# A ring of four 4 MB weight homes and a transposed gather of two experts at once, in the mixture-of-experts loop of a hybrid decoder step

## What is computed

```python
def moe(h, w_router, b_router, w_gate_up, b_gate_up, w_down, b_down):
    logits = (xt @ w_router + b_router).astype(jnp.float32)
    top_v, top_i = lax.top_k(logits, TOP_K)          # 4 of 32
    gate = jax.nn.softmax(top_v, axis=-1)
    ...
    def expert_block(args):
        xb, e = args
        gu = xb @ w_gate_up[e] + b_gate_up[e]        # 1024 x 2048
        gt, up = gu[..., :D_EXPERT], gu[..., D_EXPERT:]
        gt = jnp.minimum(gt, SWIGLU_LIMIT)
        up = jnp.clip(up, -SWIGLU_LIMIT, SWIGLU_LIMIT)
        act = (up + 1) * (gt * jax.nn.sigmoid(gt * SWIGLU_ALPHA))
        return act @ w_down[e] + b_down[e]           # 1024 x 1024
```

## Time and profile before

| | us |
|---|---|
| median of 3 runs | 1392.07 (1383.91 to 1394.49) |
| the profiled execution, its own time | 1394.99 |
| its span in the trace | 1393.2 |
| start of the first expert's gate/up on TensorE | 460.23 |
| end of the last expert's down projection | 1379.80 |
| last weight issue by SyncE | 1336.8 |
| TensorE busy (share of the span) | 1316.5 (94%) |
| VectorE, ScalarE busy | 377.2 (27%), 259.2 (19%) |
| bytes moved | 459.93 MB, 330 GB/s over the span |

### The profile page before, as it was taken

One profiled execution on the slowest core, in us unless ns is written; L12 is line 12 of the kernel. 1 busy time (PEld: TensorE's weight loads), 2 busy tenths in 40 slices (PEclk: granted clock), 3 DMA queues, 4 the chain that ended last, 5 costly groups with the idle time before them and its releaser, 6 DMA issues.

```text
span 1393.2 us, 16949 instructions
## 1 busy us (share of the span) xinstructions
PE 1316.5 (94%) x6704; PEld 627.8 (45%) x6704; DVE 377.2 (27%) x705; ACT 259.2 (19%) x473; POOL 79.6 (6%) x48
## 2 busy tenths in 40 slices
PE   6999969798889999999999999999999999999996
PEld 5888846797745333333333333333333333333332
DVE  3043765975453211111112111121112111121112
ACT  2113433122202111111111111121111111111112
POOL 0000151360000000000000000000000000000001
PEclk9999978898897899999999999999999999999998
DMA  8356673013458699999999999999999999999994
GB/s 263 133 158 166 227 210 79 4 44 124 156 188 341 247 415 428 429 428 429 428 429 428 429 429 429 429 429 428 429 429 429 429 428 429 428 429 428 429 429 168
DMA packets 52505, 459.93 MB, mean 330 GB/s; under 512 B 7922, under 2 KB 10300, under 8 KB 27884
## 3 DMA queue, kind: packets, MB, share of 16 engines
q1 hardware_dynamic: 49252, 451.45, 78.6%
q0 software_dynamic: 1888, 5.34, 2.0%
q10 hardware_dynamic: 1328, 2.64, 0.6%
HBM read 454.27 MB, written 5.11 MB: 330 GB/s over the span
## 4 chain that ended last, share of the span: by engine, by line
PE 83%; DMA 6%; DVE 4%; issue 3%; ACT 2%; POOL 1%; SPq 1%; ACTq 0%; DVEq 0%; POOLq 0%
PE ps L1688 30%; PE ps L1715 15%; PE ps L1290 8%; PE ps L1651 4%; PE ps L1636 4%; PE ps L1673 4%; PE ps L1421 3%; DMA work<-in_w_gate_up 2%; DMA ring<-in_w_gate_up 2%; PE ps L1549 2%; PE ps L1265 2%; PE ps L1643 2%; ACT work L703 1%; DVE ring L826 1%; PE ps L1490 1%
## 5 line engine op out<-in xcount | busy, mean ns | idle before, releaser
L1688 PE MATMUL ps<-ring,work 128*64 128x512 f32 x1536 | 338.5, 596 | 2.5 <-DMA ring<-in_w_gate_up 1.6
L1688 PEld LDWEIGHTS ps<-ring,work 128*64 128x64 f32 x1536 | 108.3, 137 | 229.3 <-issue 225.1
L1715 PE MATMUL ps<-ring,work 128*64 128x512 f32 x768 | 170.1, 595 | 0.0
L1290 PE MATMUL ps<-work,ring 128*128 128x264 f32 x672 | 152.0, 389 | 0.4 <-DVE work L826 0.4
L1200 DVE TENSOR_SCALAR work<-ps 128x512 f32<-128x512 f32 x32 | 22.2, 692 | 437.1 <-PE ps L1688 437.1
L1290 PEld LDWEIGHTS ps<-work,ring 128*128 128x128 f32 x672 | 128.6, 192 | 22.7 <-DVE work L826 0.5
L1218 DVE SCALAR_TENSOR_TENSOR work<-work 128x512 f32<-128x512 f32 x32 | 24.1, 752 | 348.1 <-ACT work L735 348.1
L1688 PE MATMUL ps<-work 128*64 128x512 f32 x512 | 113.2, 594 | 0.5 <-DMA work<-in_w_gate_up 0.5
L1715 PEld LDWEIGHTS ps<-ring,work 128*64 128x64 f32 x768 | 53.0, 137 | 115.4 <-issue 115.4
L726 ACT ACTIVATE work<-work 128x512 f32<-128x512 f32 x32 | 20.2, 632 | 442.6 <-DVE work L1200 442.6
L826 DVE TENSOR_TENSOR work<-work 128x512 f32<-128x512 f32 (+8 forms) x79 | 62.4, 790 | 52.7 <-ACT work L518 46.7
(11 more groups left out here) (263 smaller groups left out, 1086.6 us busy)
## 6 DMA issues: line engine op xcount, KB each, us to landing
ring<-in_w_gate_up SPq DMA_DIRECT2D x96, 2048.0 KB, 21.5
ring<-in_w_down SPq DMA_DIRECT2D x48, 2048.0 KB, 25.7
work<-in_w_gate_up SPq DMA_DIRECT2D x32, 2048.0 KB, 22.2
work<-in_w_down SPq DMA_DIRECT2D x16, 2048.0 KB, 26.3
ring<-in_w_in SPq DMA_DIRECT2D x6, 3072.0 KB, 15.8
ring<-in_w_out SPq DMA_DIRECT2D x1, 4096.0 KB, 14.3
ring<-in_w_in SPq DMA_DIRECT2D x2, 1536.0 KB, 8.7
ring<-in_cache_k SPq DMA_DIRECT2D x16, 192.0 KB, 3.3
```

Source lines behind the costliest of these rows:

```text
L1290: last = mm(psum(job, T), WIN[gi % 2][:, k, j * 128:(j + 1) * 128], hT[:, k, :], start=k == 0, stop=k == KD - 1)
L1688: last = mm(PS[bnk][g * 64:g * 64 + 64, :], lhs, UNIT[n % 8][:, w0 + base + g * 512:w0 + base + (g + 1) * 512], start=False, stop=k == KD - 1)
L1715: last = mm(PS[BY][g * 64:g * 64 + 64, :], lhs, UNIT[n % 8][:, w0:w0 + 512], start=k == 0, stop=k == KD - 1)
```

## The change

**Homes and pieces.** The ring becomes four homes of 4 MB at the same total of 16 MB. A unit of gate/up is 4 rows of 8 KB for each partition, 32 KB in a row; two units an expert. The down weights of an expert are one unit, of two pieces of 16 KB for each partition, as before. Three units an expert, twelve in a group of four experts. `unit_used` is raised once a unit, so twice in gate/up, and once at the end of down. Before the loop it is raised 1, 2 and 1 times at the three places.

**Halves.** Of the twelve units of a group, n = 4 (the second gate/up unit of expert 1) goes out as two DMAs of 2 MB, the first as soon as TensorE has used the first half of unit 0 (`half_used`). Unit n = 11 (the down unit of expert 3) goes out as two DMAs with a semaphore each, so TensorE can begin on its first half.

**Gather.** `sel` now holds two experts side by side (128 tokens x 128 slots), made by VectorE at every second expert with four instructions in place of two at each. A gather is a matmul with the normed rows, every fourth column, as the stationary operand and `sel` as the moving one: its result is transposed already. One half of D for two experts is 8 matmuls of 128x128; half 0 is done in the even expert and half 1 in the odd one, for the next pair. `gather_T`, its semaphores and the copy to `xg` go; ScalarE makes one copy a half, into one of two buffers `XG`.

**Order.** The transposes of the activations and their copy now come ahead of those of the gating matrix. The four bias matmuls of the next expert stand together after down, in an order in which neighbours differ in rows and columns of the array. Between router and loop `open_sum(0)` is split: one half ahead of the wait for the gates, the other after the ranks. VectorE adds the samples' bias before it makes the gates of the prompt, and the gates' transposes use bank BY. All rows of D are spread over the partitions by four instead of by two, in the router's weights too.

The diff, cut to its core:

```diff
-        UNIT = [view(RING, 4096 * 5, 4096), view(RING, 4096 * 4, 4096), view(RING, 4096 * 3, 4096), view(RING, 4096 * 2, 4096),
-                view(WORK, 13256, 4096), view(WORK, 24504, 4096), view(RING, 0, 4096), view(RING, 4096, 4096)]
+        UNIT = [view(RING, 8192 * 2, 8192), view(RING, 8192, 8192), view(WORK, 20408, 8192), view(RING, 0, 8192)]
...
-        xg = place(512)
-        xgT = place(4, 128)
+        XG = [place(2, 4, 2, SLOT), view(WORK, 17576, 2, 4, 2, SLOT)]
...
-            def load_experts(first, it):
+            def load_experts(first, it, turn4):
 
                 for j in range(4):
-                    for u in range(6):
-                        n = 6 * j + u
-                        sp.wait_ge(S_("unit_used"), it * 6 + n + 1)
-                        if u < 4:
-                            src = wgu[bass.ds(first + j, 1), u * 256:(u + 1) * 256, :].rearrange("a (p j) n -> p (a j n)", j=2)
+                    for u in range(3):
+                        n = 3 * j + u
+                        unit, done = UNIT[n % 4], S_(f"ld_u{n % 4}")
+                        if u < 2:
+                            src = wgu[bass.ds(first + j, 1), u * 512:(u + 1) * 512, :].rearrange("a (p j) n -> p (a j n)", j=4)
                         else:
-                            src = wdn[bass.ds(first + j, 1), (u - 4) * 512:(u - 3) * 512, :].rearrange("a (p j) n -> p (a j n)", j=4)
-                        sp.dma_start(UNIT[n % 8], src).then_inc(S_(f"ld_u{n % 8}"), 16)
+                            src = wdn[bass.ds(first + j, 1)].rearrange("a (u p j) n -> p (a u) (j n)", u=2, j=4)
+                            unit = unit.rearrange("p (u m) -> p u m", u=2)
+                        if n == 4:
+                            sp.wait_ge(S_("half_used"), turn4 + 1)
+                            sp.dma_start(unit[:, 0:4096], src[:, 0:4096]).then_inc(S_("ld_half"), 16)
+                        elif n == 11:
+                            sp.wait_ge(S_("unit_used"), it * 3 + n + 1)
+                            sp.dma_start(unit[:, 0:1], src[:, 0:1]).then_inc(S_("ld_down_half"), 16)
+                        sp.wait_ge(S_("unit_used"), it * 3 + n + 1)
+                        rest = slice(1 if n == 11 else 0, 2) if u == 2 else slice(4096 if n == 4 else 0, 8192)
+                        sp.dma_start(unit[:, rest], src[:, rest]).then_inc(done, 16)
...
+            def gathered(P, half, count):
+
+                act.wait_ge(S_("xg_full"), count)
+                nc.scalar.activation(XG[P % 2][:, half, :, :, OWN:SLOT],
+                                     PS[BX][:, :].rearrange("p (c e s) -> p c e s", c=4, e=2)[:, :, :, OWN:SLOT], ACT.Copy)\
...
+                with act.Fori(0, NE // 4) as q:
+                    for j in range(4):
+                        it = act.snap(p * NE + q * 4 + j)
+                        act.wait_ge(S_("gt"), it + 1)
+                        nc.scalar.activation(sg, gt, ACT.Sigmoid, scale=ALPHA).then_inc(S_("sg"), 1)
+                        gathered(j // 2 + 1, j % 2, it + 3)
+                        act.wait_ge(S_("actT_full"), it + 1)
+                        nc.scalar.activation(actT, PS[BG][:, :].rearrange("p (c s) -> p c s", c=4), ACT.Copy).then_inc(S_("actT_out"), 1)
+                        act.wait_ge(S_("selgT_full"), it + 1)
+                        nc.scalar.activation(selgT, PS[BY][:, 0:256], ACT.Copy).then_inc(S_("selgT_out"), 1)
+                        act.wait_ge(S_("samp_out"), it + 1)
+                        act.wait_ge(S_("unit_used"), it * 3 + 7)
+                        nc.scalar.activation(yS, PS[BY][:, :], ACT.Copy).then_inc(S_("y_out"), 1)
...
+                        if e_ == 0:
+                            for n in range(4):
+                                v.tensor_scalar(sel[:, n // 2, n % 2, :], C["slots"][:, 0:SLOT], posx[:, n // 2, bass.ds(it + 2 + n % 2, 1)], None,
+                                                ALU.is_equal).then_inc(S_("sel_next"), 1)
...
-            pe.sem_inc(S_("unit_used"), 3)
+            pe.sem_inc(S_("unit_used"), 1)
...
-            pe.sem_inc(S_("unit_used"), 3)
+            pe.sem_inc(S_("unit_used"), 2)
...
-            pe.sem_inc(S_("unit_used"), 2)
+            pe.sem_inc(S_("unit_used"), 1)
...
+            open_sum(1, 0)
+            open_sum(1, 1)
             h2_T(2)
             logits(1)
+            open_sum(0, 0)
             pe.wait_ge(S_("gate"), 1)
...
-            open_sum(0)
...
+            open_sum(0, 1)
...
-            def gather(sem_name, count):
-                pe.wait_ge(S_(sem_name), count)
-                for m in range(2):
-                    for g in range(2):
-                        last = mm(PS[BX][g * 64:g * 64 + 64, :], sel[:, m, :], h2[:, m, g * 512:(g + 1) * 512],
-                                  start=m == 0, stop=m == 1)
+            def gather(half):
+
+                for c in range(4):
+                    for m in range(2):
+                        last = mm(PS[BX][:, c * 128:(c + 1) * 128], h2[:, m, half * 512 + c:(half + 1) * 512:4],
+                                  sel[:, m].rearrange("p e s -> p (e s)"), start=m == 0, stop=m == 1)
                 last.then_inc(S_("xg_full"), 1)
 
-            def gather_T(it):
-                pe.wait_ge(S_("xg_out"), it + 1)
-                for c in range(4):
-                    last = nc.tensor.transpose(PS[BX][:, c * 128:(c + 1) * 128], half(xg, c // 2, c % 2), C["ident"])
-                last.then_inc(S_("xgT_full"), 1)
-
-            def bias(i, count):
+            def bias(count):
 
                 pe.wait_ge(S_("pick"), count)
-                for g in range(2):
+                for i, g in ((0, 0), (1, 1), (0, 1), (1, 0)):
                     q = slice(i * NE, (i + 1) * NE)
                     mm(PS[(BG, BU)[i]][g * 64:g * 64 + 64, :], pick[q, :], ebias[q, g * 512:(g + 1) * 512], start=True, stop=False)
 
-            gather("sel", 1)
+            pe.wait_ge(S_("sel"), 1)
+            gather(0)
             bank_free(BU)
             bank_free(BG)
             pe.wait_ge(S_("ld_ebias"), 32)
-            bias(0, 1)
-            bias(1, 1)
-            gather_T(0)
+            bias(1)
+            pe.wait_ge(S_("xgT_out"), 1)
+            gather(1)
...
                 pe.wait_ge(S_("xgT_out"), it + 1)
                 for k in range(KD):
-                    n, w0 = 6 * j + k // 2, (k % 2) * 2048
-                    if k % 2 == 0:
-                        pe.wait_ge(S_(f"ld_u{n % 8}"), turn4 * 48 + 16 * (n // 8 + 1))
+                    if k == 4 and j % 2 == 0:
+                        pe.wait_ge(S_("xgT_out"), it + 2)
+                    n, w0 = 3 * j + k // 4, (k % 4) * 2048
+                    if k % 4 == 0:
+                        if n == 4:
+                            pe.wait_ge(S_("ld_half"), turn4 * 16 + 16)
+                        pe.wait_ge(S_(f"ld_u{n % 4}"), turn4 * 48 + 16 * (n // 4 + 1))
                     h_, c_ = k // 4, k % 4
-                    lhs = xgT[:, c_, h_ * 64:h_ * 64 + 64]
+                    lhs = XG[j // 2][:, h_, c_, j % 2, :]
                     for bnk, base in ((BG, 0), (BU, 1024)):
                         for g in range(2):
                             last = mm(PS[bnk][g * 64:g * 64 + 64, :], lhs,
-                                      UNIT[n % 8][:, w0 + base + g * 512:w0 + base + (g + 1) * 512], start=False, stop=k == KD - 1)
-                    if k % 2:
+                                      UNIT[n % 4][:, w0 + base + g * 512:w0 + base + (g + 1) * 512], start=False, stop=k == KD - 1)
+                    if k == 1 and j == 0:
+                        last.then_inc(S_("half_used"), 1)
+                    if k % 4 == 3:
                         last.then_inc(S_("unit_used"), 1)
                 combine(it)
-                gather("sel_next", it * 2 + 2)
+                if j % 2 == 0:
+                    pe.wait_ge(S_("sel_next"), it * 2 + 4)
+                pe.wait_ge(S_("xgT_out"), it + 2)
+                gather(j % 2)
+                pe.wait_ge(S_("act"), it + 1)
+                for c in range(4):
+                    last = nc.tensor.transpose(PS[BG][:, c * 128:(c + 1) * 128], up[:, c:512:4], C["ident"])
+                last.then_inc(S_("actT_full"), 1)
                 pe.wait_ge(S_("selg"), it * 2 + 2)
                 for m in range(2):
                     last = nc.tensor.transpose(PS[BY][:, m * 128:(m + 1) * 128], selg[:, m, :], C["ident"])
                 last.then_inc(S_("selgT_full"), 1)
-                gather_T(it + 1)
-                pe.wait_ge(S_("act"), it + 1)
-                for c in range(4):
-                    last = nc.tensor.transpose(PS[BG][:, c * 128:(c + 1) * 128], up[:, c:512:4], C["ident"])
-                last.then_inc(S_("actT_full"), 1)
-
-                bias(1, it + 2)
+
                 pe.wait_ge(S_("selgT_out"), it + 2)
                 pe.wait_ge(S_("actT_out"), it + 1)
+                n = 3 * j + 2
+                if j == 3:
```

(25 more changed lines are left out.)

122 lines of the change are left out of this document (50 added, 72 removed).

## The result

The changed kernel takes **1415.51 us** (median of 4 runs, 1412.76 to 1418.67), the one before, run beside it, 1389.52 (4 runs, 1383.91 to 1394.49): a ratio of 1.018, 95% interval 1.015 to 1.021. Slower, where 1390 (1381 to 1400) was forecast. The profiled execution took 1415.79 (span 1413.8), 20.8 over that of before, 1394.99.

The account below looks back on a forecast made before the run. DMA was taken as the bound: last idling, then bytes over rate, then TensorE's tail. Issue +2.6, rate -7.1 and tail +2.4 summed to -2.1 us, giving 1390.0 us on the median's scale, range 1381 to 1400.

Parts of the forecast that it names:

- The gather: Between gate/up and down: 8 matmuls of 128x128 at 0.27 us each, 2.1 us, bounds 1.9 to 4.5.
- X: TensorE's time from the end of gate/up to down in each expert: 5.8 us, against 6.72 before.
- The bound: In the loop: DMA binds; TensorE's period of 27.7 us stays under the 28.6 at which the periods cross.
- Rival (c): In the loop: TensorE becomes the bound through a gather above 3.1 us; 1437 us at the 4.5 bound; chance 6%.
- The rate: Gate/up DMA from unit 6 on: 32 KB pieces save 14.8 ns fixed cost a piece, -7.1 us.
- Issue and start: Loop's beginning: first expert starts at 460.5; the issue ending DMA's idling moves to 488.8, +2.6 us.
- rival (b): Before the first expert: the clock stays up or rises earlier, -6.5 us, 1383.5; chance 16%.
- The tail: From the last gate/up unit's landing to the end of down: 19.8 us against 17.4, +2.4 us.
- The biases: After each expert's down: all four bias matmuls together take 1.0 us.
- What would show it: Trace signs: 431 to 432 GB/s, period 27.7 then 29.1 us, TensorE waiting about 1.5 us at second gate/up units.
- Rival (e): In the loop: TensorE's DMA waits of about 1.5 us an expert drop the clock; not priced, no chance given.

Follow-up runs that it names:

- a1_contig: The changed kernel with h2 stored sorted by VectorE, so the gather reads its stationary operand without a stride: 1391.41 us, ratio 0.9996 to the kernel before.
- five f32 loads above: Gather's stationary load at steps of 4, 8, 12, 16 and 32 bytes, in five kernels, the changed one among them: 192, 196, 262, 330 and 335 ns.
- e6_stride3: `a1_contig` with the gather's stationary operand read at a step of three f32 elements (wrong columns, same work): 1395.73 us, one run.
- a4_contig_16k: `a1_contig` with gate/up in 16 KB pieces instead of 32 KB and h2 sorted by two: 1398.86 us, ratio 1.0055 to the kernel before.
- b1_halves: `a1_contig` with units 6 and 10 of each four experts also fetched in halves: 1391.98 us, ratio 1.0003 to the kernel before.
- b2_gather_only: The kernel before, its ring kept, with only the change's two-expert gather (stride two), new order and biases together: 1386.06 us, ratio 0.9967.
- bf16 runs: `a1_contig` with the gather reading h2 and sel as bf16 at steps of 4, 8, 16 bytes (wrong columns): 1389.89, 1393.32, 1387.39 us, one run each.
- a2_16k_stride2: The changed kernel with gate/up in 16 KB pieces, so the gather reads every second column: 1393.59 us, ratio 1.0016 to the kernel before.
- a3_ring_only: The kernel before with only the change's ring of four 4 MB homes and its pieces, old gather kept: 1394.42 us, ratio 1.0023.
- e5_stride8: `a1_contig` with the gather's stationary operand read at a step of eight f32 elements (wrong columns, same work): 1413.02 us, one run.

## Why the prediction was wrong, point by point

- **The gather, the step that failed.** It was 2.1 us (bounds 1.9 to 4.5), is 3.94 to 4.01, near the upper end. The row taken, had shape, type and engine right, and columns side by side. The row that seemed to clear the stride, the activations' transposes, was of another kind. At the same step its load takes 213 ns, the gather's 330; the gating transposes of the same kernel, whose columns lie side by side, load in 147 ns:

```profile
L1708 PEld LDWEIGHTS ps<-work x128: 196/213/302, 480.5 to 1391.9; 128*128 128x128 f32 x128
```

```profile
L1712 PEld LDWEIGHTS ps<-work 128*128 128x128 f32 x64 | 8.4, 147 | 0.0
```

  So the step has its price there too, but hardly in the spacing of the records, which is all that the prediction looked at: transposes follow each other by 0.12 us with the step and by 0.11 without. The gather's records follow each other by 0.11 us side by side (`a1_contig`) and by 0.23 at a step of four. Its spacing grows with its load at every step: 0.11, 0.12, 0.17, 0.23 and 0.24 us for the five f32 loads above. Why a transpose pays so much less than a matmul for the same step stays open.
- **X, gate/up to down.** Forecast 5.8, after 7.28 to 7.55; at the right price of the gather the forecast would have been 5.8 + 3.94 - 2.1 = 7.6. With no stride it is 5.34 and 5.53, so the copies behind the gather were put 0.3 to 0.4 too dear: from its end to down it is 1.4 us (510.21 + 1.40 = 511.61), not 1.8. ScalarE starts each copy before the last has ended: at 510.21, 510.68 and 511.18, for 0.54, 0.60 and 0.38 us.
- **The bound.** Rival (c), held at 6%, is what happened. Its threshold, periods crossing at 28.6 us, fits the runs on either side: `e6_stride3` at 28.4 ends on a DMA wait, the change at 29.39 on TensorE. Loop start 460.98 + 32 x 29.39 - 1.02 = 1400.4, which the trace has at 1400.3: 20.5 later than before, the 20.8 of the result. The error was in one input and its chance, not in the mechanism.
- **The rate.** This term was mis-sized too: -7.1 us forecast, -3.7 measured (`a1_contig` against `a4_contig_16k`), and in the changed kernel nothing of it shows, since DMA doesn't bind. Two sizes, one of them from another tensor with other rows, don't give the slope between the next two.
- **Issue and start.** Forecast 460.5 and 488.8, measured 460.98 and 489.6: near, but in part by luck, since errors cancel. The two gathers took 4.03 and 3.93 instead of 3.6, and X was 1.7 longer; against that the clock was up for expert 0's gate/up (13.91 for 15.52), which rival (b) had in part.
- **The tail** was 19.8, and `a1_contig`, where DMA binds, has 19.5. **The biases** were 1.0, measured 1.02.
- **What would show it.** "I am wrong if TensorE never waits for DMA after the middle of the loop" was the right test, and was met.
- **Rival (e)**, waits that drop the clock, did not arise in the change, where TensorE never waits for DMA in the loop. It did in `b1_halves` (last section).

## What to carry to other kernels

Before a weight layout is made for longer DMA pieces, look at what it does to the step with which TensorE reads the *other* operand: at 16 bytes or more a f32 stationary load went from 192 to 330 ns, and with matmuls of 128 columns their spacing doubled. Whether longer matmuls would hide it no run here shows. Take the price of a new access pattern from a row with that pattern in the same kind of instruction; where no such row exists, the chance of the far bound is not 6%. And when two engines' periods stand within 3% of each other, a busy share or a rate in GB/s can't tell which is the bound: the releaser of the first matmul of a unit and the time from issue to landing can.

## What the runs showed of the hardware

- The load at a step of four f32 doesn't follow TensorE's clock. In the change, at a granted clock of 0.50 (443 to 460 us), both gathers' 16 loads took 3.81 us in all, and 3.81 at 1.00. Side by side they do: `a1_contig`'s 16 loads ahead of the loop, at 0.50, took 3.49 us where 16 at full clock took 1.86. At 0.50 steps of two (`b2_gather_only`) and three (`e6_stride3`) took the same 3.49, so at the lower clock only the step of four stood out, and by 9%.
- The clock can fall around a wait for DMA. In `b1_halves` TensorE waits 2.7 us for a gate/up unit five times in the loop, and at three of these, within 1 us of where it resumes, the granted clock falls to 0.50 for 3.4 us:

```profile
914.00:918.00 4.00, 1.27 (x8) 0.37 (x6) 0.00 (x0) 0.00 (x0) 0.00 (x0) 1.00 1.02 434
918.00:922.00 4.00, 4.00 (x12) 1.37 (x11) 0.00 (x0) 0.00 (x0) 0.00 (x0) 0.57 0.98 418
```

  The traces with f32 gathers whose longest wait is 1.9 us or less, `a1_contig` with 22 waits over 0.9 us among them, show no such fall in the loop. The bf16 runs, whose longest waits are 2.5 us, have 9 to 12 such stretches, and two of the five waits of `b1_halves` have none, so the length of a wait is not all that decides.
- The start of the loop scatters by 15 us between profiled executions, 450.3 to 464.8, and the clock ahead of it goes with that in part. Windows of `a2_16k_stride2` (its loop starts at 455.9) and of `a1_contig` (463.1):

```profile
444.00:452.00 8.00, 7.72 (x54) 4.77 (x53) 5.80 (x28) 2.54 (x10) 0.00 (x0) 1.00 0.67 285
```

```profile
444.00:452.00 8.00, 7.01 (x37) 5.22 (x35) 2.34 (x14) 4.63 (x12) 0.00 (x0) 0.68 0.79 338
452.00:460.00 8.00, 8.00 (x27) 4.25 (x30) 6.48 (x28) 0.46 (x1) 0.00 (x0) 0.50 0.00 1
```

  Kernels with a clock of 1.00 there are early, `a3_ring_only` (450.3), `e5_stride8` (455.6) and `a2_16k_stride2`; most with a stretch at 0.50 are later: before (460.2), the change, `a1_contig` and `a4_contig_16k`. But `b2_gather_only` starts at 453.9 with 13.7 us at 0.50 (437 to 451), so the clock is not all of it. This is why the loop's length, and not the end, was compared above. That it also spreads the runs of one kernel over 11 us and more is likely, but no trace shows it. What decides the clock there stays open.
- A write of VectorE at a step of 512 bytes costs: 128x512 f32 sorted by four took 1.10 us, two of them 2.2 us for the one of 128x1024 before, 1.28.
